# Four small moves on TensorE, one on the scalar engine's DMA queue, and a shorter sum in the router of a decoder block

## What is computed

```python
z = rms_norm(x, g_mix) @ w_in + b_in                  # 5376 columns: conv pair, q, k, v, two gates
u = causal_depthwise_conv(a * sigmoid(b), conv_w) + conv_b   # conv_w is [31, 1024]
y_conv = silu(layer_norm(u)) @ w_conv_out + b_conv_out
y_attn = attention(q, k, v) @ w_attn_out + b_attn_out
x = x + (gate_conv * y_conv + gate_attn * y_attn) @ w_out
hf = rms_norm(x, g_ffn)
logits = hf @ w_router + b_router                     # 32 experts
top_w, top_e = softmax(top_k(logits, 4))
g = minimum(hf[tokens of e] @ w_gate[e] + b_gate[e], 7)
u = clip(hf[tokens of e] @ w_up[e] + b_up[e], -7, 7)
y[tokens of e] += top_w * (((u + 1) * g * sigmoid(1.702 * g)) @ w_down[e] + b_down[e])
out = rms_norm(x + y, g_final)
```

## Time and profile before

| | us |
|---|---|
| median of 3 runs | 1174.55 (1174.53 to 1174.64) |
| the profiled execution | 1175.73 |
| its span, first to last instruction | 1174.0 |
| TensorE busy | 1127.8 (96%) |
| vector engine busy | 325.8 |
| scalar engine busy | 179.8 |
| moved by DMA | 441.69 MB, mean 376 GB/s |

### The profile page before, as it was taken

The page is one execution under the profiler, slowest core; times in us unless marked ns, Lnnn a source line. Parts: engine busy times, 40 slices in busy tenths (PEclk is TensorE's granted clock), DMA queues, the critical chain, the costliest instruction groups (busy, mean ns, idle before and its releaser), DMA issues.

```text
span 1174.0 us, 13697 instructions
## 1 busy us (share of the span) xinstructions
PE 1127.8 (96%) x5333; PEld 534.3 (46%) x5333; DVE 325.8 (28%) x792; ACT 179.8 (15%) x351; POOL 33.6 (3%) x39
## 2 busy tenths in 40 slices
PE   8999999999999999999999999999999999999997
PEld 6888887854333333333333333333333333333332
DVE  2999963424111111111211111111111111111111
ACT  2111375122011000010110110110000000000011
POOL 2350000000000000000000000000000000000000
PEclk9999999998999999999999999999999999999999
DMA  9965434678999999999999999999999999999996
GB/s 287 348 208 172 143 143 180 251 282 307 415 405 428 434 429 433 430 429 432 434 432 430 431 431 432 434 433 429 431 432 432 435 431 430 430 433 433 433 421 263
DMA packets 54565, 441.69 MB, mean 376 GB/s; under 512 B 4231, under 2 KB 34185, under 8 KB 37640
## 3 DMA queue, kind: packets, MB, share of 16 engines
q1 hardware_dynamic: 52720, 439.89, 90.5%
q0 software_dynamic: 432, 0.95, 0.4%
q10 hardware_dynamic: 1384, 0.44, 0.2%
HBM read 440.08 MB, written 1.05 MB: 376 GB/s over the span
## 4 chain that ended last, share of the span: by engine, by line
PE 91%; DMA 5%; another core or an unknown queue 2%; ACT 1%; DVE 1%; issue 0%; SPq 0%; ACTq 0%; DVEq 0%
PE bank L1454 54%; PE bank L1193 17%; PE bank L1422 5%; PE bank L1407 4%; DMA arena<-in_w_up 4%; PE bank L1318 2%; PE bank L1490 2%; PE bank L1461 1%; PE bank L1414 1%; PE bank L1497 1%; DMA arena<-in_w_in 1%; PE bank L1350 1%; PE bank L1216 1%; PE bank L1231 0%
## 5 line engine op out<-in xcount | busy, mean ns | idle before, releaser
L1454 PE MATMUL bank<-arena,x_columns 128*64 128x512 f32 x2048 | 462.6, 596 | 21.5 <-DMA arena<-in_w_up 20.7
L1454 PEld LDWEIGHTS bank<-arena,x_columns 128*64 128x64 f32 x2048 | 147.7, 137 | 290.7 <-issue 268.0
L1454 PE MATMUL bank<-arena,act_columns 128*64 128x512 f32 x1024 | 227.7, 597 | 9.9 <-DMA arena<-in_w_down 9.4
L1193 PE MATMUL bank<-arena 128*128 128x256 f32 x928 | 206.0, 383 | 0.7 <-DMA arena<-in_w_in 0.7
L1193 PEld LDWEIGHTS bank<-arena 128*128 128x128 f32 x928 | 176.4, 192 | 26.8 <-issue 1.7
L1454 PEld LDWEIGHTS bank<-arena,act_columns 128*64 128x64 f32 x1024 | 78.9, 138 | 155.0 <-issue 154.3
L820 DVE SCALAR_TENSOR_TENSOR arena<-arena x240 | 96.4, 480 | 0.1
L1045 DVE TENSOR_SCALAR bias_selector<-ones_bf,expert_onehot 96x64 bf16<-96x64 bf16 x32 | 7.6, 236 | 270.8 <-PE bank L1414 270.8
L1079 DVE TENSOR_SCALAR gate_clipped<-bank 128x512 f32<-128x512 f32 x32 | 22.1, 692 | 202.8 <-PE bank L1454 202.8
L1083 DVE TENSOR_SCALAR hidden<-bank 128x512 f32<-128x512 f32 x32 | 22.1, 692 | 189.8 <-PE bank L1454 189.8
L1422 PE MATMUL bank<-y_block,scatter 64*128 64x512 f32 x256 | 63.6, 615 | 0.7 <-ACT y_block L702 0.7
(11 more groups left out here) (186 smaller groups left out, 494.5 us busy)
## 6 DMA issues: line engine op xcount, KB each, us to landing
arena<-in_w_up SPq DMA_DIRECT2D x25, 4096.0 KB, 46.4
arena<-in_w_down SPq DMA_DIRECT2D x25, 4096.0 KB, 47.5
arena<-in_w_gate SPq DMA_DIRECT2D x24, 4096.0 KB, 45.2
arena<-in_w_in SPq DMA_DIRECT2D x21, 1024.0 KB, 11.8
arena<-in_w_gate SPq DMA_DIRECT2D x10, 2048.0 KB, 13.9
arena<-in_w_up SPq DMA_DIRECT2D x8, 2048.0 KB, 12.4
arena<-in_w_down SPq DMA_DIRECT2D x7, 2048.0 KB, 16.5
arena<-in_w_down SPq DMA_DIRECT2D x13, 1024.0 KB, 9.0
```

The costliest lines, as they stand in the source:

```text
L1193: last = pe.matmul(bank[n % 3][:, j * T:(j + 1) * T], w[:, c, j * P:(j + 1) * P], src[:, c, :], start=(c == 0), stop=(c == C - 1))
L1454: last = pe.matmul(dst[h * CAP:(h + 1) * CAP, :], lhs(row), cols(rows[:, row, :], h), start=(row == 0), stop=(row == MROWS - 1))
```

## The change

- Scalar queue: `conv_w` is issued ahead of the seven vectors.
- Attention: `project(GATE0 + 5)` is cut in two and its first half goes ahead of `scores(1)`; `project(CONV0 + 3)` is cut in four, with its first quarter ahead of `turn_probs(3, (0, 1))` and its last behind `attend(3)`.
- Router, second half of the tokens: chunks 4 to 7 take the tokens as the weights and w_router as the moving side, and sum straight in `LOGITS[1]`, which is now in bank 2. Only chunks 0 to 3 go by the parts; `sum_of_parts(1)` adds them in the middle of that sum. `logits_in_parts(1)` on the vector engine moves ahead of `gained_columns(1, 2)`. The second normalisation on the scalar engine waits for `logit_done` and no more for `parts_done`.
- Expert 0: its gate and up go to banks 0 and 1 (`FIRST_A`, `FIRST_B`) and are begun by their biases, before and after `ranks(1)`, ahead of the products. `bias_select(0)` moves from the first gather's evacuation to the start of the vector engine's part in the router.
- `start_y` is called with a row and puts one of its four matmuls after rows 0, 2, 4 and 6 of expert 0's down.

```diff
@@ scalar @@
+            act.dma_start(cwrows, t_in["conv_w"]).then_inc(cw_loaded, 16)
             for name, (row, rows) in VEC.items():
                 if name != "g_mix":
                     act.dma_start(vrows[row:row + rows, :], t_in[name].rearrange("(c p) -> c p", p=P)).then_inc(vecs_loaded, 16)
-            act.dma_start(cwrows, t_in["conv_w"]).then_inc(cw_loaded, 16)
...
-                act.wait_ge(parts_done, t + 1)
+                act.wait_ge((parts_done, logit_done)[t], t + 1)
@@ vector @@
+            bias_select(0).then_inc(first_bias, 1)
...
             gained_columns(1, 1)
+            logits_in_parts(1)
             gained_columns(1, 2)
             new_sum(1)
-            logits_in_parts(1)
...
-                bias_select(0)
@@ tensor @@
+            project(GATE0 + 5, hT, (0,))
             scores(1)
-            project(GATE0 + 5, hT)
+            project(GATE0 + 5, hT, (1,))
...
+            project(CONV0 + 3, cen, (0,), chunks=FIRST)
             turn_probs(3, (0, 1))
-            project(CONV0 + 3, cen, (0,), chunks=FIRST)
+            project(CONV0 + 3, cen, (0,), chunks=REST)
             turn_probs(3, (2,))
-            project(CONV0 + 3, cen, (0,), chunks=REST)
+            project(CONV0 + 3, cen, (1,), chunks=FIRST)
             attend(3)
-            project(CONV0 + 3, cen, (1,))
+            project(CONV0 + 3, cen, (1,), chunks=REST)
...
+                    if t == 1 and c >= 4:
+                        summed = pe.matmul(LOGITS[t], hfT[t][:, c, :], wrt[:, c, :], start=(c == 4), stop=(c == C - 1))
+                        if c == C - 1:
+                            summed.then_inc(logit_done, 1)
+                    else:
+                        last = pe.matmul(LOGIT_PARTS[t][rows, :], wrt[:, c, :], hfT[t][:, c, :],
+                                         start=(c < 4), stop=(c >= 4 or t == 1))
...
+            def first_biases(dst, bias, h):
+                pe.matmul(dst[h * CAP:(h + 1) * CAP, :], bsel[:], by_half(bias, h), start=True, stop=False)
...
             router_logits(1, 1)
+            sum_of_parts(1)
             router_logits(1, 2)
-            sum_of_parts(1)
-            first_gather(0, range(5))
+            first_gather(0, range(4))
+            pe.wait_ge(bias_cut, PARTS)
+            pe.wait_ge(first_bias, 1)
+            first_biases(FIRST_A, bgate, 0)
+            first_biases(FIRST_A, bgate, 1)
             ranks(1)
-            first_gather(0, range(5, C))
+            first_gather(0, range(4, C))
+            first_biases(FIRST_B, bup, 0)
+            first_biases(FIRST_B, bup, 1)
             first_gather(1)
...
-            def start_y():
-
-                pe.wait_ge(wT_out, 1)
-                pe.wait_ge(bdown_loaded, 16)
-                for t in range(TT):
-                    for h in range(2):
-                        pe.matmul(Y[t][h][:], wT[:, t * P:(t + 1) * P], bdown[:, h * 512:(h + 1) * 512],
-                                  start=True, stop=False)
+            def start_y(row):
+                if row == 0:
+                    pe.wait_ge(wT_out, 1)
+                    pe.wait_ge(bdown_loaded, 16)
+                if row % 2 == 0:
+                    t, h = divmod(row // 2, 2)
+                    pe.matmul(Y[t][h][:], wT[:, t * P:(t + 1) * P], bdown[:, h * 512:(h + 1) * 512],
+                              start=True, stop=False)
...
-                product(DN, n, lambda c: actT[:, c % 4, c // 4, :], None, cycle)
+                product(DN, n, lambda c: actT[:, c % 4, c // 4, :], None, cycle, between=start_y if n == 4 else None)
```

More of the change, by code:

```diff
@@ L289, in build @@
                          [bank[(5, 7)[c // 4]][:, c % 4 * CAP:(c % 4 + 1) * CAP] for c in range(C)]]
-        LOGITS = [bank[4][:, 128 + t * NE:128 + (t + 1) * NE] for t in range(TT)]
+        LOGITS = [bank[4][:, 128:128 + NE], bank[2][:, 0:NE]]
         x_loaded = [sem(f"x_loaded{t}") for t in range(TT)]
@@ L1011, in ranked, with bias_select @@
                 dv.tensor_scalar(sel[:, t, :], iota[:, 0, :], rank[:, t, 0:1], None, ALU.is_equal).then_inc(sel_ready, 1)
+            def bias_select(b):
+                return dv.tensor_scalar(bsel[:], ones_h[0:PARTS * NE, 0:CAP], ehot[:, bass.ds(b, 1)], None, ALU.mult)
             dv.wait_ge(bias_cut, PARTS)
@@ L1042, in select @@
                 last.then_inc(sel_ready, 1)
-            def bias_select(b):
-                dv.tensor_scalar(bsel[:], ones_h[0:PARTS * NE, 0:CAP], ehot[:, bass.ds(b, 1)], None, ALU.mult)
             def tokensT(b):
@@ L1067, in first_tokensT, with moe_block @@
                                             first_half[:, c, :], ALU.mult, ALU.add).then_inc(xT_ready, 1)
-            def moe_block(b, then_gather=True, lead=LEAD):
+            def moe_block(b, then_gather=True, lead=LEAD, gate=A, up=B):
                 if then_gather:
@@ L1078, in moe_block @@
                 dv.wait_ge(piece_done, b * MPE + (FRONT - lead + EW))
[L1079 removed]
+                dv.tensor_scalar(gmin, gate[:], LIMIT, None, ALU.min).then_inc(gmin_ready, 1)
                 dv.wait_ge(sig_ready, b + 1)
@@ L1108, in _ @@
             dv.tensor_copy(wT, DN[PARTS * NE:P, 0:T]).then_inc(wT_out, 1)
-            moe_block(0, lead=0)
+            moe_block(0, lead=0, gate=FIRST_A, up=FIRST_B)
             with dv.Fori(1, NE - 1) as b:
@@ L1336, in router_logits @@
                     rows = slice(c % 4 * NE, (c % 4 + 1) * NE)
-                    last = pe.matmul(LOGIT_PARTS[t][rows, :], wrt[:, c, :], hfT[t][:, c, :],
-                                     start=(c < 4), stop=(c >= 4))
-                if hi == D:
+                    if t == 1 and c >= 4:
[5 more added lines that the diff above has]
+                                         start=(c < 4), stop=(c >= 4 or t == 1))
+                if t == 0 and hi == D or t == 1 and k == 0:
                     last.then_inc(parts_done, 1)
@@ L1344, in sum_of_parts @@
                 pe.wait_ge(ident4_ready, 1)
-                pe.matmul(LOGITS[t], logit_parts[:, t, :], ident4[:], start=True, stop=True).then_inc(logit_done, 1)
+                last = pe.matmul(LOGITS[t], logit_parts[:, t, :], ident4[:], start=(t == 0), stop=(t == 0))
+                if t == 0:
+                    last.then_inc(logit_done, 1)
             def add_x(t, h):
@@ L1433, in row_arrived, with product @@
                                landed(n, row) if cycle is None else cycle * 16 + (landed(n, row) - 16 * LOOP0))
-            def in_half(flat, h):
-                return flat[:, h * 512:(h + 1) * 512]
-            def by_half(flat, h):
-                return flat.rearrange("q (p h k) -> q h p k", h=2, k=EROWS)[:, h]
-            def product(dst, n, lhs, bias=None, cycle=None, halves=(0, 1), ready=None):
+            def product(dst, n, lhs, bias=None, cycle=None, halves=(0, 1), ready=None, begun=False, between=None):
                 rows = matrix_rows(n)
@@ L1454, in product @@
                             last = pe.matmul(dst[h * CAP:(h + 1) * CAP, :], lhs(row), cols(rows[:, row, :], h),
-                                             start=(row == 0), stop=(row == MROWS - 1))
+                                             start=(row == 0 and not begun), stop=(row == MROWS - 1))
                         if row in ROWS_USED.get(n, ()):
                             last.then_inc(rows_done, 1)
-                    last.then_inc(piece_done, 1)
-                    if i == 0 and bias is not None:
+                        if k == EROWS - 1:
+                            last.then_inc(piece_done, 1)
+                        if between is not None:
+                            between(row)
+                    if i == 0 and bias is not None and not begun:
                         for h in range(2):
```

17 lines of the change are left out of this document (10 added, 7 removed).

## The result

The changed kernel's median was 1177.97 us (20 executions, 1173.01 to 1179.93) against 1173.9 us for the kernel before on the same chip (20 executions, 1167.0 to 1176.33): a ratio of 1.004, 95% interval 1.0026 to 1.0054. (The ratios here are not quotients of the medians: each lies within 0.0005 of the quotient of the means.) It is slower, by more than the bound of 0.2%. The time lies at the upper edge of the forecast range; the centre, 1175.25 us, and its "within 0.2%" were wrong.

What follows compares the result with a forecast made beforehand. After about 285 us DMA sets the end; before, TensorE sets the first refill. Terms -1.8 + 3.2 + 0.3 - 1.0 = +0.7 us gave a median of 1175.25 us (1176.4 profiled), range 1171.7 to 1178.3, within 0.2% at chance 0.55.

Steps and rivals of the forecast that it cites:

- The premise: DMA sets the end after about 285 us, so a microsecond at the first refill is a microsecond at the end.
- Part 1: Attention splits: projection pieces fill TensorE's waits of 0.6 and 1.2 us, a gain of 1.8 us.
- Part 2: conv_w ahead of the vectors: its 31 rows on one DMA engine delay them, TensorE waits, a loss of 3.2 us.
- Rival A: Slower: the clock falls to 0.5 in the new wait, costing 1.0 to 2.7 us more; 1177.3 us typical, chance 0.24.
- Rival B: Faster: the vectors don't share conv_w's engine, so its reordering costs 0; 1172.05 us, chance 0.12.
- Part 3: Router and first expert up to the first refill: a loss of 0.3 us, with the gather at half clock.
- Rival C: Faster: bias pairs and changed timing keep the clock at 1.00 through the gather; 1171.95 us, chance 0.09.
- Part 4: Biases of down spread over a down product: loads issued earlier deepen the DMA queue, a gain of 1.0 us.
- the work stays the same: Spreading the biases of down was taken to leave the amount of work as it was in one block.

Runs made afterwards that it cites:

- before_p1: The kernel before, file unchanged, profiled once more: 1167.66 us, mean clock 1.0.
- conv_back: The changed kernel with conv_w's load issued behind the seven vectors again: 1168.4 us, ratio 0.9979 to the kernel before.
- before_p2: The kernel before, file unchanged, another profiled execution: 1173.79 us, mean clock 0.994.
- splits_alone: The kernel before with only the two splits in the attention: 1167.2 us, ratio 0.9972.
- conv_first_alone: The kernel before with only conv_w's load put ahead of the seven vectors: 1180.26 us, ratio 1.0071.
- changed_again: The changed kernel itself, unaltered, on a third chip: 1174.64 us, ratio 1.003 to the kernel before.
- router_alone: The kernel before with only the change of the router and of expert 0: 1171.98 us, ratio 1.0013.
- spread_alone: The kernel before with only the biases of down spread over expert 0's down: 1170.4 us, ratio 1.0007.
- changed_down_block: conv_back with the biases of down in one block again: 1166.67 us, ratio 0.9967 to the kernel before.
- conv_split: The changed kernel with conv_w still ahead, but as two loads of 16 and 15 rows: 1167.05 us, ratio 0.9963 to the kernel before.
- split_and_block: conv_split with the biases of down in one block again: 1166.14 us, ratio 0.9955 to the kernel before.
- warm_wait: The changed kernel with seven unneeded matmuls ahead of the wait for the vectors: 1174.59 us, ratio 1.0024 to the kernel before.

## Why the prediction was wrong, step by step

The span, cut at four marks that each timeline shows: the start of the vectors' transpose, the issue of the first refill, and the landing of the 5th and of the 27th load from that refill on. Each column is the stretch up to that mark in us. "Falls" are those at the gather and behind it; in all profiles the clock also falls in the last 3 to 7 us.

| kernel | transpose | to first refill | to 5th landed | to 27th landed | to the end | span |
|---|---|---|---|---|---|---|
| before, both falls | 19.23 | 256.79 | 15.76 | 62.31 | 819.87 | 1174.0 |
| before_p1, no fall | 16.70 | 254.90 | 14.12 | 60.69 | 819.49 | 1165.9 |
| after | 23.63 | 253.63 | 13.90 | 61.38 | 819.18 | 1171.7 |
| conv_back, no fall | 17.34 | 252.15 | 13.50 | 61.15 | 819.67 | 1163.8 |

Set against the execution of the same kind, before_p1, the changed kernel is 5.8 us slower, and this closes: +6.9 up to the transpose, -1.3 up to the refill, +0.2 behind it. The -1.3 is nearly the sum of -1.9 (splits), -0.3 (router part), -0.5 (no wait for conv_w) and +1.35 (projection 1, at half clock until 26.6 us), which is -1.35.

**The premise held.** What the kernel needs from the 27th load on is the same in these four within 0.7 us (819.2 to 819.9; the largest of all profiles is 820.8, in before_p2), and a microsecond won or lost ahead of the first refill is found again in the span.

**Part 1 was right**, -1.8 us: both waits are gone, with nothing late behind them, and the stretch to the refill is 1.9 us shorter in splits_alone. The timing bears this out less plainly. Its interval, 0.9954 to 0.9991, holds 1.9 us (0.9984); but the executions at full mean clock are only 0.6 us quicker (means 1167.1 and 1167.7 us on the same chip), and part of the ratio comes from 10 of 12 having it against 18 of 33. Over all chips the share stands out: the seven kernels here that have the splits, and no undivided conv_w ahead of the vectors, show full mean clock in 59 of 84 executions, more than the kernel before on each of the three chips and in all (34 of 97). With 5.6 us between the kinds that is some 2 us of the mean, an estimate from these numbers, as much as the two waits. My sum had no such term. Why the splits change the share isn't explained; it may be the moment at which TensorE comes to the gather.

**Part 2 is the step that failed, in its size.** The mechanism was the right one: one engine, 31 rows, the vectors behind them. The sum said "vectors at 21.6 to 22.9 us, less TensorE at 19.23 us, I take 3.2". Both numbers were off. The vectors came at 23.6, 22.6, 23.1 and 23.3 us in the four profiles that have the reordering. In the changed kernel conv_w's 31 packets ran from 13.46 to 21.38 us, 7.9 us as I had said, but from 0.6 us later. Behind them, on that engine, came 9 of the vectors' 90 rows, the last until 22.41 us, where the other 81 had been through by 16.35. Then it took another 1.2 us until the transpose started, for which I had allowed 0.3 to 1.0. The queue of the changed kernel in 16.4 to 21.4 and in 21.4 to 22.5 us:

```profile
q10 hardware_dynamic: 18, 0.07, 5.1%
...
q10 hardware_dynamic: 17, 0.00, 1.9%
```

The wait was 3.4 us longer than my 3.2. An arrival at 23.63 us, and not at the 22.4 us that stand behind the 3.2, is 1.2 us of this. The other 2.2 us are TensorE's: the 19.23 us were no property of the kernel, but what one execution showed whose clock rose late. In the profiles of executions with no matmuls added at the start the clock rises between 7.6 and 14.4 us, and projection 0 takes from 7.2 us to 9.2. In 12 of the 17 profiles TensorE was ready for the transpose at 16.7 to 17.4 us, in the other five at 18.7 to 20.0. The profile that I started from had the sign of it, in two projections of the same 32 records; the record of the clock begins only with its rise, at 14.3 us there, and the stretch of 0 to 30 us shows 1.00 all the same:

```profile
10.20 9.19 PE L1193 MATMUL bank<-arena 128*128 128x256 f32 x32 [0.69 <-DMA arena<-in_w_in]
...
19.32 7.10 PE L1193 MATMUL bank<-arena 128*128 128x256 f32 x32
```

As the vectors' arrival doesn't move with it, the wait is the difference: 6.63, 5.48 and 3.17 us were seen. What was a cushion of nothing for a slow start is a lost start for a quick one. Priced by runs of the full change the reordering costs 0.6% (conv_back), alone 0.7%, not the 0.27% that I took.

**Rival A was the nearest**, at 0.24: the clock does fall in the wait, every time it was seen, at waits of 6.63, 5.48 and 3.17 us. Its price of 1.0 to 2.7 us nearly holds too (projection 1 took 1.35 us more than 7.09 in the changed kernel, 2.6 in conv_first_alone, 2.8 in changed_again). The Trainium skill (TensorE: Matmul & The Clock Gate, "HAM oscillation — how this bites in real kernels") says that a wait for a DMA of about this length sends the clock back; I gave that too little weight against the row in which waits of 1.7 us didn't. The runs agree with the page, at 3.17 us and above. Its place in my sum, on top of a wait of 3.2 us, was too low by the error of part 2. That its 1177.3 us lies near the measured 1177.97 is partly luck: it stood for a loss of 2.75 us, the medians differ by 4.07, and the kernel before was 0.65 us quicker this time than in the three runs that I started from. Rival B is refuted by conv_first_alone and by the nine rows behind conv_w.

**Part 3 was right as "nothing that shows"**: -0.3 us with the clock up (252.47 us to the refill in splits_alone, 252.15 in conv_back) and 1.0013 in timing. With the clock down, which was the case of my +0.3, it is 257.5 us in router_alone (258.05 less a wait of 0.57 for conv_w), against 256.8 to 257.3 in the three profiles of the kernel before with the falls. Rival C, the clock staying up at the gather, did happen in the changed kernel's profile, but nothing shows this part as its cause: router_alone lost the clock there in its profile, and the kernel before keeps it there in a third of its executions.

**Part 4 was wrong**: it earned nothing, 1.0007 alone and not my -1.0 us. For executions without full mean clock the means are 1173.5 us in spread_alone and 1173.6 before, on the same chip. And I forgot the executions that keep the clock: there the spread costs about 1 us in all three pairs (1168.6 against 1167.7 in spread_alone, 1167.3 against 1166.2 in conv_back and changed_down_block, 1167.2 against 1166.0 in conv_split and split_and_block; the last two pairs are from different chips, on which the kernel before differs by 0.1 us). The second fall of the clock is worth less than it looked: from the first refill to the end it takes 895.6 to 898.0 us in the profiles with both falls, 896.0 to 896.5 with the one at the gather alone and 894.0 to 895.7 with none. And that the block brings it about isn't shown. Of the eight profiles with the block and a fall at the gather six have a second one, conv_first_alone and split_and_block don't; the two with the spread (spread_alone, warm_wait) don't either. My premise "the work stays the same" was wrong too, as the changed kernel's timeline shows:

```profile
311.83 1.12 PE L1499 MATMUL bank<-conv_w_rows_then_biases,y_block 32*128 32x512 f32 x2
...
312.88 1.94 PE L1478 MATMUL bank<-arena,act_columns 128*64 128x512 f32 x8
...
314.75 1.12 PE L1499 MATMUL bank<-conv_w_rows_then_biases,y_block 32*128 32x512 f32 x2
```

A bias pair and eight product records take 2.92 us (311.83 to 314.75); eight product records by themselves are half of the 3.63 us that sixteen take, 1.8. So a pair costs 1.1 us and four of them 4.4, where the block took 3.70 in before_p1. From the first of the 40 records of the biases and of expert 0's down to the next step it takes 10.65 us in before_p1, as a block, and 11.80 in the changed kernel (310.84 to 322.64), both at full clock:

```profile
305.76 3.70 PE L1470 MATMUL bank<-conv_w_rows_then_biases,y_block 32*128 32x512 f32 x8
309.39 7.09 PE L1454 MATMUL bank<-arena,act_columns 128*64 128x512 f32 x32
316.41 0.75 PE L1490 MATMUL bank<-ident,hidden 128*128 128x128 f32 x4
```

That these 1.15 us are what the executions lose fits the sizes; it wasn't tested by itself.

**What stays open**: why the same kernel's clock rises at 7.6 us in one execution and at 14.4 us in another, and what decides at the gather. In the profiles the two don't go together simply: before_p2 rose early and fell at the gather, conv_split started late and didn't. I also have no profile of the changed kernel's slower kind, 12 of 20 executions; that it has the fall at the start and one at the gather is inferred from its mean clock of 0.992 to 0.994, and from conv_first_alone, whose profile has both and a mean of 0.993.

## What to carry to other kernels

Before a load is moved ahead on a queue, look at its outer size: one that can't be divided runs through one engine, and all that is queued behind it comes late by its whole time. Cut at row 16, the load here took 1.8 to 2.5 us and not 7.9; what is queued behind it still comes later by about that much, which can be a wait where the engine is early. Before an arrival is set against "when the engine gets there", ask how that time varies from one execution to the next; one profile gives one value, and the slack in it may belong to a slow start. Three agreeing times can be all of one kind, so compare executions by their mean granted clock before a difference of 0.3% is explained.

## What the runs showed of the hardware that I had not expected

The same program loses the clock at the same place in some executions and keeps it in others: 6.8 us at half clock at the gather and 3.4 us behind that, or nothing, and 5.6 us of total time between the two kinds. Three of the four profiles of the kernel before show the falls, and by their mean clock 63 of 97 executions had them. Idle time does not decide it: ahead of the gather TensorE idled 0.75 us in three short waits in before_p1 and before_p2 alike, and one kept the clock; in warm_wait it was busy for 5.96 of the 6.00 us ahead of the fall, and for 20.00 of 20.00 around the second fall in before_p2. What ran there was thin work, fp32 gather records of 64 columns and weights of 32 rows. So work almost without a pause doesn't keep the clock by itself, while seven wide matmuls in a wait of 6.6 us did. And one row decides over the number of DMA engines: 31 rows took 7.9 us through one engine, and cut into 16 and 15 they took 1.8 to 2.5 us; ahead of the vectors they left a wait of 0.66 us in one of two profiles and none in the other.
